# Context spectrum ahead of the last z tile, row copies on ScalarE, and a new engine order in the Hyena stage of a two-layer diffusion step

## What is computed

```python
def bidir_long_conv(u, h, bias):
    L, C = u.shape[1], u.shape[2]
    g = jnp.concatenate([h[:, 0], jnp.zeros((1, C), jnp.float32), h[:0:-1, 1]], axis=0)
    U = jnp.fft.rfft(u, n=2 * L, axis=1)
    G = jnp.fft.rfft(g, n=2 * L, axis=0)
    y = jnp.fft.irfft(U * G[None], n=2 * L, axis=1)[:, :L]
    return y + u * bias
...
    z = centred_dwconv(z, lp['hy_conv_w'], lp['hy_conv_b'])
    x0, x1, u = jnp.split(z, 3, axis=-1)
    y = bidir_long_conv((x1 * u).astype(jnp.float32), h, lp['hy_bias'].astype(jnp.float32))
    return x0 * y.astype(z.dtype)
```

## Time and profile before

| what | value |
|---|---|
| median of 3 runs | 2029.27 us (2028.94 to 2031.91) |
| the profiled execution's own time | 2029.84 us |
| its span, first to last instruction | 2026.9 us |
| PE busy | 1963.9 us (97%) |
| DVE busy | 1168.8 us (58%) |
| ACT busy | 740.6 us (37%) |
| POOL busy | 195.6 us (10%) |
| mean granted TensorE clock | 0.992 |

### The profile page before, as it was taken

The page is one execution under the profiler, slowest core; times in us unless marked ns, Lnnn a source line. Parts: engine busy times, 40 slices in busy tenths (PEclk is TensorE's granted clock), DMA queues, the critical chain, the costliest instruction groups (busy, mean ns, idle before and its releaser), DMA issues.

```text
span 2026.9 us, 30168 instructions
## 1 busy us (share of the span) xinstructions
PE 1963.9 (97%) x12914; PEld 1881.4 (93%) x12914; DVE 1168.8 (58%) x1743; ACT 740.6 (37%) x1098; POOL 195.6 (10%) x210
## 2 busy tenths in 40 slices
PE   8899998999999999999999999899999999999997
PEld 3599997999999999999989999899998999999996
DVE  7824559787477677767455456953347343243435
ACT  3534444422273321333244445532227332133313
POOL 0320001100150000000121000110015000000011
PEclk9999999999999999999999999899999999999999
DMA  8431012255213335443322101212221211221121
GB/s 329 154 116 66 16 56 99 99 189 185 85 63 128 143 141 196 153 166 120 106 73 100 48 27 61 84 60 92 78 79 63 84 63 65 91 84 63 64 72 53
DMA packets 37438, 203.39 MB, mean 100 GB/s; under 512 B 4294, under 2 KB 7927, under 8 KB 19256
## 3 DMA queue, kind: packets, MB, share of 16 engines
q1 hardware_dynamic: 30904, 181.37, 25.1%
q0 software_dynamic: 3312, 13.35, 1.9%
q10 hardware_dynamic: 3088, 6.75, 0.9%
HBM read 193.31 MB, written 8.14 MB: 99 GB/s over the span
## 4 chain that ended last, share of the span: by engine, by line
PE 83%; DVE 10%; ACT 4%; issue 2%; ACTq 0%; DMA 0%; POOL 0%; SPq 0%; DVEq 0%
PE gemm_psum L618 51%; PE gemm_psum L648 15%; PE gemm_psum L671 3%; PE gemm_psum L631 3%; PE aux_psum L758 2%; PE gemm_psum L691 2%; PE aux_psum L739 2%; PE aux_psum L747 1%; ACT h_src_rows L1186 1%; PE gemm_psum L525 1%; DVE aux_psum L1793 1%; PE gemm_psum L563 1%; DVE w_lo L1618 1%; DVE x L1797 1%; PE aux_psum L545 1%
## 5 line engine op out<-in xcount | busy, mean ns | idle before, releaser
L618 PE MATMUL gemm_psum<-h_hi,w_hi 128*128 128x322 f32 x2144 | 497.1, 313 | 0.3
L618 PE MATMUL gemm_psum<-h_hi,w_lo 128*128 128x322 f32 x2144 | 493.5, 311 | 0.0
L618 PE MATMUL gemm_psum<-h_lo,w_hi 128*128 128x322 f32 x2144 | 491.3, 310 | 0.0
L618 PEld LDWEIGHTS gemm_psum<-h_hi,w_hi 128*128 128x128 f32 x2144 | 362.8, 189 | 4.4 <-issue 3.1
L618 PEld LDWEIGHTS gemm_psum<-h_lo,w_hi 128*128 128x128 f32 x2144 | 362.1, 189 | 0.0
L618 PEld LDWEIGHTS gemm_psum<-h_hi,w_lo 128*128 128x128 f32 x2144 | 361.9, 189 | 0.0
L1618 DVE TENSOR_TENSOR w_lo<-w_raw,w_hi 128x2048 fp32r<-128x2048 f32 (+4 forms) x128 | 244.6, 1911 | 182.1 <-ACT w_hi L1116 181.1
L1116 ACT ACTIVATE w_hi<-w_raw 128x2048 fp32r<-128x2048 f32 (+4 forms) x128 | 204.1, 1594 | 170.7 <-PE gemm_psum L648 65.6
L1525 DVE CUSTOM_DVE_ANT_0 aux_psum<-w_raw,cond_by_row 128x1024 f32<-128x1024 f32 x160 | 191.0, 1257 | 5.0 <-DMA w_raw<-in_ada_t 4.7
L1751 DVE SCALAR_TENSOR_TENSOR x<-gemm_psum,mod,x 128x128 f32<-128x128 f32 (+2 forms) x144 | 55.4, 434 | 158.7 <-PE gemm_psum L648 128.9
L648 PE MATMUL gemm_psum<-act_hi,w_lo 128*128 128x322 f32 x616 | 141.9, 312 | 0.0
(11 more groups left out here) (349 smaller groups left out, 3264.5 us busy)
## 6 DMA issues: line engine op xcount, KB each, us to landing
w_raw<-in_w_up SPq DMA_DIRECT2D x44, 1024.0 KB, 4.8
w_raw<-in_ada_t SPq DMA_DIRECT2D x42, 1024.0 KB, 4.7
w_raw<-in_w_down SPq DMA_DIRECT2D x32, 704.0 KB, 4.1
w_raw<-in_w_gate SPq DMA_DIRECT2D x16, 1024.0 KB, 4.8
w_raw<-in_w_z SPq DMA_DIRECT2D x12, 1024.0 KB, 4.7
w_raw<-in_w_out SPq DMA_DIRECT2D x8, 1024.0 KB, 4.7
ada_early<-in_ada SPq DMA_DIRECT2D x4, 1024.0 KB, 19.4
g_kept<-g_rows_out POOLq DMA_DIRECT2D x8, 512.0 KB, 4.4
```

The costliest lines, as they stand in the source:

```text
L618: last = mm(gp[:, 2 * (t % 2) + hf, 0:HALF], w[:, off + P * kk:off + P * (kk + 1)], moving(kk, lo)[:, hf * HALF:(hf + 1) * HALF], start=kk ...
```

## The change

Four things are done. On PE, spectrum 0 is placed ahead of the last z tile, spectrum 1 no longer waits for that tile's copy, and the four tiles of the attention projection are spread: two before the context's inverse, one between it and spectrum 3, one after spectrum 4. The banks are renumbered for it. On ACT, the copies of row 0 come in from DVE (`y_high`), and the order becomes: y of pair 0, split gF1, `u_hi(5, 9)`, rows of the attention projection 0 and 1, y of pair 1, row 2, the two copies of spectrum 3, y of pair 2, row 3, splits gI and gG. On DVE, the products of pair 0 move ahead of `u_lo(3, 5)`, of the split of gA and of the x0 taps; the context's result (line 1914) moves ahead of the products of pair 2; and the split of gI moves between the products of pairs 3 and 4.

```diff
-    spec_bank = lambda r: ax[:, r, :] if r < 2 else gp[:, r % 4, :]
+    spec_bank = lambda r: ax[:, r, :] if r < 2 else gp[:, (r - 2) % 4, :]
-    EARLY_BANKS = [(1, 2), (1, 0), (1, 2), (1, 0)]
+    EARLY_BANKS = [(1, 2), (1, 0), (1, 0), (1, 0)]
...
             to_features(NB - 1)
-            pe.wait_ge(sem["at_lo"], due("at_lo", NB - 1))
-            tile(9, 1, KD, KD * P, h_mov, "z_mm")
             pe.wait_ge(sem["us_ready"], due("us_ready", 1))
             pe.wait_ge(sem["ut_out"], due("ut_out", 5))
             spectrum(0, U_V[0])
+            pe.wait_ge(sem["at_lo"], due("at_lo", NB - 1))
+            tile(9, 1, KD, KD * P, h_mov, "z_mm")
+            pe.wait_ge(sem["us_ready"], due("us_ready", 3))
+            spectrum(1, U_V[1])
             pe.wait_ge(sem["z_acc"], due("z_acc", 12))
-            for p_ in range(1, 3):
-                pe.wait_ge(sem["us_ready"], due("us_ready", 1 + 2 * p_))
-                spectrum(p_, U_V[p_])
+            pe.wait_ge(sem["us_ready"], due("us_ready", 5))
+            spectrum(2, U_V[2])
...
             attn_projected(1)
-            for n in (2, 3):
-                pe.wait_ge(sem["pa_out"], due("pa_out", n - 1))
-                attn_projected(n)
...
             last.then_inc(sem["cinv_mm"], raised("cinv_mm"))
+            pe.wait_ge(sem["pa_out"], due("pa_out", 2))
+            attn_projected(2)
             pe.wait_ge(sem["us_rest"], due("us_rest", 4))
             spectrum(3, U_V[3])
             spectrum(4, U_V[4])
+            pe.wait_ge(sem["pa_out"], due("pa_out", 3))
+            attn_projected(3)
...
+            def y_high(p_):
+                for o in range(2):
+                    src = us[:, o, :] if p_ < 3 else (us, prod)[o][:, p_ - 3, :]
+                    if p_ < 2:
+                        act.wait_ge(sem["y_src"], due("y_src", 2 * p_ + o + 1))
+                        run(us[0:1, o, :], prod[0:1, 1 - o, :], ACT.Copy).then_inc(sem["act_order"], raised("act_order"))
+                        act.wait_ge(sem["act_order"], now("act_order"))
+                    hi(yhi[:, Y_SLOT[p_], 1 - o, :], src, "y_src", 2 * p_ + o + 1, "y_hi")
             act.wait_ge(sem["usp_mm"], due("usp_mm", 4))
+            y_high(0)
             split(gF1)
...
+            u_hi(5, 9)
+            early_row(0)
+            early_row(1)
+            y_high(1)
+            early_row(2)
+            for o in range(2):
+                act.wait_ge(sem["usp_mm"], due("usp_mm", 7 + o))
+                run(ureg[:, 2 * o, :], spec_bank(6 + o), ACT.Copy).then_inc(sem["odd_out"], raised("odd_out"))
+            act.wait_ge(sem["cinv_mm"], due("cinv_mm", 1))
+            y_high(2)
+            early_row(3)
+            split(gI)
+            split(gG)
+            for p_ in (3, 4):
+                act.wait_ge(sem["linv_mm"], due("linv_mm", p_ - 2))
+                y_high(p_)
...
             u_lo(1, 3)
-            x0_tap(1, 0)
-            u_lo(3, 5)
-            x0_tap(1, 2)
-            split(gA)
-            for p_ in range(3):
...
-                real = p_ < 2
...
-                    V.tensor_copy(us[0:1, 0, :], prod[0:1, 1, :]).then_inc(sem["y_src"], raised("y_src"))
...
-                    V.tensor_copy(us[0:1, 1, :], prod[0:1, 0, :]).then_inc(sem["y_src"], raised("y_src"))
...
+            products(0)
+            u_lo(3, 5)
+            split(gA)
+            x0_tap(1, 0)
+            x0_tap(1, 2)
+            y_low(0)
+            split(gF1)
+            products(1)
+            y_low(1)
             dve.wait_ge(sem["cinv_mm"], due("cinv_mm", 1))
...
+            products(2)
+            y_low(2)
...
+                if at == 0:
+                    split(gI)
```

More of the change, by code:

```diff
@@ L1316, in _ @@
             split(gA)
-            u_hi(5, 9)
             def early_row(n):
@@ L1876, in _, with products @@
             u_lo(1, 3)
-            x0_tap(1, 0)
-            u_lo(3, 5)
-            x0_tap(1, 2)
-            split(gA)
-            for p_ in range(3):
+            def products(p_):
                 gr, gi = gsp[:, G_SLOT[p_], 0, :], gsp[:, G_SLOT[p_], 1, :]
                 ur, ui = spec_bank(2 * p_), spec_bank(2 * p_ + 1)
-                dve.wait_ge(sem[("g_first_in", "g_first_in", "g_mid_in", "g_odd_in", "g_last_in")[p_]], 16 * (L + 1))
+                dve.wait_ge(sem[("g_first_in", "g_first_in", "g_mid_in")[p_]], 16 * (L + 1))
+                if p_:
+                    dve.wait_ge(sem["y_ready"], due("y_ready", 2 * p_))
                 dve.wait_ge(sem["usp_mm"], due("usp_mm", 2 * p_ + 1))
                 TT(prod[:, 0, :], ur, gr, ALU.mult).then_inc(sem["dve_order"], raised("dve_order"))
-                if p_:
-                    dve.wait_ge(sem["y_ready"], due("y_ready", 2 * p_))
                 TT(us[:, 0, :], ur, gi, ALU.mult).then_inc(sem["usp_out"], raised("usp_out"))
@@ L1894, in _, with y_low @@
                 dve.wait_ge(sem["dve_order"], now("dve_order"))
+                TT(us[:, 0, :], us[:, 0, :], us[:, 1, :], ALU.add).then_inc(sem["y_src"], raised("y_src"))
                 dve.wait_ge(sem["usp_out"], now("usp_out"))
-                real = p_ < 2
-                TT(us[:, 0, :], us[:, 0, :], us[:, 1, :], ALU.add).then_inc(sem["dve_order" if real else "y_src"], raised("dve_order" if real else "y_src"))
-                if real:
-                    dve.wait_ge(sem["dve_order"], now("dve_order"))
-                    V.tensor_copy(us[0:1, 0, :], prod[0:1, 1, :]).then_inc(sem["y_src"], raised("y_src"))
                 dve.wait_ge(sem["y_src"], now("y_src"))
-                TT(us[:, 1, :], prod[:, 0, :], prod[:, 1, :], ALU.subtract).then_inc(sem["dve_order" if real else "y_src"], raised("dve_order" if real else "y_src"))
-                if real:
-                    dve.wait_ge(sem["dve_order"], now("dve_order"))
-                    V.tensor_copy(us[0:1, 1, :], prod[0:1, 0, :]).then_inc(sem["y_src"], raised("y_src"))
+                TT(us[:, 1, :], prod[:, 0, :], prod[:, 1, :], ALU.subtract).then_inc(sem["y_src"], raised("y_src"))
+            def y_low(p_):
                 for o in range(2):
-                    ys = Y_SLOT[p_]
-                    lo(ylo[:, ys, 1 - o, :], us[:, o, :], yhi[:, ys, 1 - o, :], "y_hi", 2 * p_ + o + 1, "y_ready")
-                if p_ == 0:
-                    split(gF1)
-            split(gI)
+                    src = us[:, o, :] if p_ < 3 else (us, prod)[o][:, p_ - 3, :]
+                    lo(ylo[:, Y_SLOT[p_], 1 - o, :], src, yhi[:, Y_SLOT[p_], 1 - o, :], "y_hi", 2 * p_ + o + 1, "y_ready")
+            products(0)
[7 more added lines that the diff above has]
+            y_low(1)
             dve.wait_ge(sem["cinv_mm"], due("cinv_mm", 1))
@@ L1940, in _ @@
             for p_ in (3, 4):
-                for o in range(2):
-                    lo(ylo[:, Y_SLOT[p_], 1 - o, :], (us, prod)[o][:, p_ - 3, :], yhi[:, Y_SLOT[p_], 1 - o, :],
-                       "y_hi", 2 * p_ + o + 1, "y_ready")
+                y_low(p_)
             split(gG)
```

22 lines of the change are left out of this document (1 added, 21 removed).

## The result

The changed kernel takes 2036.34 us (median of six runs, 2035.69 to 2037.73), the kernel before 2029.20 beside it on the same chip (six runs, 2028.82 to 2032.05). The ratio is 1.0031, with a 95% interval from 1.0021 to 1.0041: slower. The medians lie 7.1 us apart; the ratio, which is not the quotient of the two medians, comes to 6.3 us. The forecast was 2033.7, in a range from 2027.5 to 2038.0. The profiled execution took 2036.08 us; its span is 2034.1 and that of before 2026.9, 7.2 us more.

What follows compares the result with a forecast made beforehand. The prediction took DVE to bound the Hyena stage; its last low half of y would come 2.2 us later a layer, +4.4 in two, giving 2034.2 on the profiled 2029.84, or 2033.7 against the median, range 2027.5 to 2038.0.

Steps and rivals of the forecast that it cites:

- PE ahead of the z tile: On PE, spectrum 0 waits about 1.8 us for ACT's fifth copy, and the last z tile ends 4.8 us later.
- Products of pair 0 and what DVE waits for next: 7.7 us leave DVE's later chain; DVE resumes 5.3 us later, at 304.2, and idles about 1.1 us for gA.
- POOL on DVE's back: POOL's four low halves of u hold DVE's SBUF-only instructions: 2.9 us of stalls, bounds 0 and 5.5.
- first rival: PE's path alone: POOL and DVE hardly meet, spectrum 3 sets the rest; +1.65 us a layer, 2032.6; chance 0.35.
- the start of the sums: DVE's sums of pair 3, also written S: forecast at 328.5 in layer 0 against 328.43 before, a shift of 0.0.
- The row copies on ACT: ACT takes 0.6 us per copy; free beside pair 0, about 1.3 us of DVE waiting for pair 1.
- The split of gI, +2.2: On DVE this 2.2 us split was done before the sums of pair 3; now it stands between pairs 3 and 4.
- What is hidden: Inverses behind PE's idle 5.6 us end by 351.8, covered until DVE's third row of h; uncovered cost under 1.5 us.
- the pivot: End of DVE's last low half of y, when POOL clears h's pads: 343.9 in layer 0, forecast 2.2 us later.
- the balance: Check of DVE's shift per layer: 5.3 later, 2.4 idle, 2.9 stalls, less 7.7, is +2.9; taken as +2.2 to +2.9.
- DVE's work as the bound: Rival: the Hyena stage shortens by the copies leaving DVE, 2.6 us a layer, to 2024.1; chance 0.15.
- More stalls: Rival: all four POOL instructions hold DVE in full, 5.5 us of stalls, +4.8 a layer, 2038.9; chance 0.10.

Runs made afterwards that it cites:

- e1: Changed kernel with the last z tile put back ahead of spectrum 0 on PE; 2030.46 us against 2030.14 for the kernel before, ratio 1.0002.
- e5: Changed kernel with spectrum 0 set inside the last z tile, ahead of its third input block; 2032.43 us against 2029.97 for the kernel before, ratio 1.0013.
- e6: Changed kernel with POOL's four low halves of u cut to 8 of 512 columns; 2036.94 us against 2029.97 for the kernel before, ratio 1.0037.
- e3: Changed kernel with the row copies put back on DVE; 2036.25 us, ratio 1.0030 to the kernel before.
- e4: Kernel before with only the row copies moved from DVE to ACT; 2030.29 us against 2030.14, ratio 1.0000.
- e2: Changed kernel with 24 matmuls of no use added in PE's gap; 2033.30 us, ratio 1.0017 to the kernel before.
- e11: Changed kernel with z tile first, 24 useless matmuls in PE's gap, ACT's pair 2 high halves ahead of spectrum 3's copies; 2029.24 us against 2030.40 for the kernel before.
- e8: Kernel before with POOL's third and fourth low half of u held until DVE has split gF1; 2028.95 us against 2029.97, ratio 0.9996.

## Why the prediction was right, and where it was not

The direction and most of the size came out as forecast. Most steps of the mechanism are borne out; one term was missing and one was too large, and they are of opposite sign, so part of the agreement is luck (see the sum).

**PE ahead of the z tile: right.** The wait for ACT's fifth copy is 1.75 us for 1.8, the spectrum starts at 291.88 for 291.9, and ACT's copy of the z tile at 302.11 for 302.15. e1 shows what this step costs: undone, S comes 1.9 us a layer earlier and the loss is gone. e5 refines it: the 1.8 us of waiting did the harm, and the 2.8 of the spectrum hardly any.

**Products of pair 0 and what DVE waits for next: right.** Products start at 295.52 (295.6), DVE resumes at 304.15 (304.2), idles 1.03 for w_hi of gA (1.1), and PE starts the attention projection at 308.82 (308.9).

**POOL on DVE's back: right in kind, 0.7 us too large.** Low half and split stalled by 2.2 us in all. The third meeting, with the add (line 1900), did not happen: it took 0.68 us, since it began at 317.63, just as POOL ended (310.62 + 7.13). The rule of the Trainium skill, page "SBUF — State Buffer", section "Who interferes with whom", that a VectorE instruction with two SBUF inputs contends with a GpSimd instruction that reads SBUF, is borne out by these rows: two SBUF inputs are held (2.59 us for 1.48 without POOL's work, e6), multiplies with one input in PSUM are not (0.68). But the prediction gave it the wrong weight. It made the stalls the difference between forecast and first rival, and e6 shows them to be worth nothing here: PE's chain through spectrum 3 arrived at the same moment. The prediction also named a wait for ACT in y_low(2) as a sign of being right; there is none, the two were level there. The forecast of 0.0 for the start of the sums came out -0.7, which is the first rival's figure (1.65 - 2.2 = -0.55), whose path this is.

**The row copies on ACT: right.** 0.61 to 0.63 us each for 0.6, with DVE waiting 0.57 + 0.49 for the 1.3 forecast. e3 and e4 show that the move neither gains nor costs anything that their intervals (some 2 us either way) can tell, in either kernel.

**The split of gI, +2.2: right.** It is 2.29 us between pairs 3 and 4, and it is most of what e2 leaves over.

**"What is hidden": the step that failed.** It said that the inverses behind PE's gap "end by 337.4 + 7.2 + 7.2 = 351.8", and that DVE needs them "only when its third row of h is done", so that a slow clock was covered. The size was fair, though low: PE's gap was 4.9 us for 5.6, the first of the two inverses behind it did run at 1.2 GHz, and the pair took 8.1 us for the 7.2 assumed. The reader was wrong. ACT's high halves of pairs 3 and 4 write the slots of pairs 1 and 2 and wait for inverses 1 and 2 (line 1352 of the changed kernel, `act.wait_ge(sem["linv_mm"], due("linv_mm", p_ - 2))`, which the kernel before has too, at its line 1331). DVE's last low halves stand behind ACT. That is 1.5 us a layer, 3.0 in all, and e2 shows it by taking it away without touching anything ahead of it. With this term, and the sums 0.7 us earlier, the pivot is +3.0 for +2.2, at the edge of the 2.2 to 2.9 that the balance gave.

**Sum.** 5.9 us in the two layers for the 4.4 forecast. The rest of the 7.2 us of the two spans is the clock at the end of the kernel: no edit stands near it, and both lengths occur among the other kernels (last section). Without the wait for the late inverses the pivot would have moved by 1.5 us a layer, +3.0 in all. That is the first rival's figure (+3.3) and not the forecast's; e2, which is this kernel, shows +2.8 in the pivots and a ratio of 1.0017. The forecast came nearer than its rival because a term that it had called hidden made up for stalls that it had counted and that were worth nothing: luck, in this part.

**The rivals.** DVE's work as the bound falls: DVE is 57% busy and has gaps of 4.76, 1.03 and 1.51 us. More stalls falls: two instructions held, not four. PE's path alone gave the start of the sums rightly and was wrong in the end, since it lacks the late inverses as the forecast does.

**What is open.** Why the clock stayed at 0.50 for 2.7 us behind one gap of 4.9 us and for over 5 behind another isn't settled; the traces show only that both occur. Nor was each part of the change tried alone: whether the high halves of pair 2 ahead of ACT's copies of spectrum 3 help the changed order by themselves was tried only together with two other edits (e11).

## What to carry to other kernels

Work moved off the engine that bounds a stage gains only where that engine has something else to do until the result is back: here four copies went to ACT and came back as waits, twice. Removing a stall pays only up to the next releaser: 2.2 us of stalls taken away gave nothing in e6, 2.1 gave 0.66 in e8. When an order is woven anew, follow every buffer slot that is written again, not only the data: a wait "until the old reader is through" turns a late or slow instruction off the path into one on it. And a gap on PE can cost twice: here the pair of inverses behind 4.9 us of idle time took 8.1 us for 5.6, and what they freed was waited for. So put the matmuls that free a slot ahead of the gap, or keep PE busy through it.
